# Start of a one-layer RG-LRU, attention and FFN kernel: gain vector through ScalarE's queue, ones first on GpSimd, twelve warm-up products, first weights in two transfers

## The reference, cut to what matters

```python
def rms_norm(x, g):
    y = x * lax.rsqrt(jnp.mean(x * x, axis=-1, keepdims=True) + EPS)
    return y * g

h = rms_norm(x, mix_norm_g[0])
proj = h @ w_in[0]                       # 1024 -> 2560
xr, yg, q, k, v = jnp.split(proj, splits, axis=-1)
...                                      # conv, RG-LRU, attention, norms
x = x + mixed @ w_out[0]
hf = rms_norm(x, ffn_norm_g[0])
up = causal_depthwise_conv(hf @ w_up[0], ffn_conv_w[0], ffn_conv_b[0])
gate, val = jnp.split(up, 2, axis=-1)
return x + (jax.nn.gelu(gate) * val) @ w_down[0]
```

## Time and profile before

| what | before |
|---|---|
| median of 3 runs | 295.36 us (295.22 to 295.43) |
| the profiled execution | 295.82 us |
| its span, first to last instruction | 294.0 us |
| TensorE busy | 287.8 us, 98% of the span |
| VectorE, ScalarE, GpSimd busy | 242.3, 201.0, 11.8 us |
| moved by DMA | 52.23 MB, mean 178 GB/s |

### The profile page before, as it was taken

How to read it: one execution, slowest core, us unless ns; L and a number is a source line. 1 busy time by engine, 2 the same in 40 slices (tenths; PEclk the granted TensorE clock), 3 DMA queues, 4 the chain that set the end, 5 groups by cost and what they waited for, 6 DMA issues and landing times.

```text
span 294.0 us, 4948 instructions
## 1 busy us (share of the span) xinstructions
PE 287.8 (98%) x1618; PEld 248.7 (85%) x1618; DVE 242.3 (82%) x443; ACT 201.0 (68%) x378; POOL 11.8 (4%) x29
## 2 busy tenths in 40 slices
PE   6999999999999999999999999999999999999996
PEld 6688999898788899888888888888888888888885
DVE  2798798898899777999978888888788888888864
ACT  4894498989695488888666666676666666776540
POOL 4000000900000000000000000000000000000000
PEclk9999999999999999999999999999999999999999
DMA  7999941231256702664746444464736544200004
GB/s 278 424 424 421 393 149 56 91 143 54 91 173 255 281 9 60 226 246 183 283 148 246 168 168 165 159 237 143 285 143 236 186 157 162 115 0 0 0 0 145
DMA packets 8111, 52.23 MB, mean 178 GB/s; under 512 B 928, under 2 KB 1312, under 8 KB 2080
## 3 DMA queue, kind: packets, MB, share of 16 engines
q1 hardware_dynamic: 7920, 51.50, 46.8%
q0 software_dynamic: 176, 0.53, 0.5%
HBM read 50.98 MB, written 1.05 MB: 177 GB/s over the span
## 4 chain that ended last, share of the span: by engine, by line
PE 94%; ACT 3%; DVE 1%; issue 1%; POOL 0%; ACTq 0%; POOLq 0%
PE bank L1353 25%; PE bank L1033 15%; PE bank L1034 15%; PE bank L1037 15%; PE bank L1357 13%; PE bank L1103 2%; PE bank L1083 1%; PE bank L1142 1%; ACT w_hi L361 1%; PE bank L1256 1%; PE bank L1169 1%; PE bank L1114 1%; DVE h_both L939 1%; PE bank L1320 1%; PE bank L1136 1%
## 5 line engine op out<-in xcount | busy, mean ns | idle before, releaser
L684 DVE TENSOR_TENSOR w_lo<-raw,w_hi 128x1024 fp32r<-128x1024 f32 x93 | 111.0, 1221 | 7.4 <-ACT w_hi L361 6.3
L361 ACT ACTIVATE w_hi<-raw 128x1024 fp32r<-128x1024 f32 x85 | 86.8, 1058 | 4.9 <-PE bank L1037 4.5
L1353 PE MATMUL bank<-h_both,w_hi 128*128 128x512 f32 x336 | 83.7, 391 | 0.6 <-ACT w_hi L361 0.6
L1353 PEld LDWEIGHTS bank<-h_both,w_hi 128*128 128x128 f32 x336 | 61.6, 188 | 12.6 <-issue 0.8
L1357 PEld LDWEIGHTS bank<-h_both,w_lo 128*128 128x128 f32 x336 | 45.8, 190 | 3.3
L1357 PE MATMUL bank<-h_both,w_lo 128*128 128x256 f32 x336 | 46.8, 282 | 0.0
L603 ACT ACTIVATE tanh_a<-bank 128x256 f32<-128x256 f32 x44 | 16.8, 381 | 40.8 <-PE bank L1357 39.9
L1033 PE MATMUL bank<-w_hi,act_hi 128*128 128x512 f32 (+1 forms) x90 | 34.8, 387 | 0.0
L1034 PE MATMUL bank<-w_lo,act_hi 128*128 128x512 f32 (+1 forms) x90 | 34.8, 387 | 0.0
L1037 PE MATMUL bank<-w_hi,act_lo 128*128 128x512 f32 (+1 forms) x90 | 34.6, 384 | 0.0
L611 ACT ACTIVATE xc<-ygate,par 128x256 f32<-128x256 f32 x44 | 26.2, 595 | 3.2 <-DVE ygate L961 3.2
(11 more groups left out here) (168 smaller groups left out, 402.8 us busy)
## 6 DMA issues: line engine op xcount, KB each, us to landing
raw<-in_stream_dram SPq DMA_DIRECT2D x47, 1024.0 KB, 4.8
x_tok<-in_x_dram SPq DMA_DIRECT2D x2, 512.0 KB, 5.1
out_dram<-x_tok SPq DMA_DIRECT2D x3, 256.0 KB, 2.3
p_T<-in_gates_dram POOLq DMA_DIRECT2D x1, 512.0 KB, 9.3
out_dram<-x_tok SPq DMA_DIRECT2D x2, 128.0 KB, 2.2
par<-in_params_dram SPq DMA_DIRECT2D x1, 117.0 KB, 6.7
mix_g<-in_params_dram POOLq DMA_DIRECT2D x1, 4.0 KB, 5.7
```

The costliest lines, as they stand in the source:

```text
L361: act.activation(w_hi[u % RING][:, :], raw_unit(u), ACT.Copy).then_inc(hi_done, 1)
L684: dve.tensor_tensor(w_lo[u % RING][:, :], raw_unit(u), w_hi[u % RING][:, :].bitcast(F32), ALU.subtract).then_inc(lo_done, 1)
L1353: pe.matmul(acc[:, :], whi[:, kc, :], h_both[:, kc, :, :].rearrange("p b t -> p (b t)"), start=kc == 0, stop=False)
```

## The change

The gain's transfer is issued by ScalarE as its first instruction, and no longer by GpSimd, so the memset of `ones` is GpSimd's first instruction in the block. `WARM_UP` goes from 10 to 12. The first 1 MB of weights goes as two transfers of 512 KB, one for each unit, with a semaphore of its own for unit 0 (`first_landed`), which `q_plain` waits for. The users of unit 1, and of all later units, still wait for `raw_landed[0]` and the others.

```diff
-WARM_UP = 10
+WARM_UP = 12
...
+        first_landed = sem("first_landed")
...
             sp.dma_start(x_tok[:, 0, :], x_t[0]).then_inc(x_landed[0], 16)
-            sp.dma_start(raw[0][:, :], stream[0]).then_inc(raw_landed[0], 16)
+            sp.dma_start(raw_unit(0), stream[0][:, 0:UNIT]).then_inc(first_landed, 16)
+            sp.dma_start(raw_unit(1), stream[0][:, UNIT:2 * UNIT]).then_inc(raw_landed[0], 16)
             sp.dma_start(x_tok[:, 1, :], x_t[1]).then_inc(x_landed[1], 16)
             sp.dma_start(par[:, :], params).then_inc(par_landed, 16)
...
         @block.gpsimd
         def _(pool):
-            pool.dma_start(mix_g[:, :], params[:, MIX_G:MIX_G + KC]).then_inc(gain_landed, 16)
             pool.memset(ones[:, :], 1.0).then_inc(ones_done, 1)
...
+            act.dma_start(mix_g[:, :], params[:, MIX_G:MIX_G + KC]).then_inc(gain_landed, 16)
             act.wait_ge(consts, 1)
             act.activation(warm_out, eps, ACT.Sqrt).then_inc(warm, 1)
...
             def q_plain(m, kc):
 
-                pe.wait_ge(raw_landed[0], 16)
+                pe.wait_ge(first_landed, 16)
                 pe.wait_ge(plain_done, PLAIN.index((m, kc)) + 1)
```

## The result

The changed kernel takes 296.36 us (median of 7 runs, 296.20 to 296.44) against 295.43 for the kernel before (7 runs, 295.04 to 295.52) on the same chip: ratio 1.0034, interval 1.0025 to 1.0043. It is 0.93 us slower. I had forecast 0.4 us faster, 294.5 to 295.5. The sign was wrong.

The account below looks back on a forecast made before the run. TensorE, nearly always busy, passes opening changes through to the end. ScalarE free at 8.38 and tile 1 at 8.2 put the square at 8.4 instead of 8.81: 295.36 - 0.4 = 294.95 us, range 294.5 to 295.5.

Parts of the forecast that it names:

- What decides: Opening, ScalarE: the new start of the square of tile 1, less 8.81, gives the change in time; -0.4 us.
- The step that failed: First 1 MB of weights: splitting it delays unit 1 and tile 1 by at most 0.2 us; 0.1 taken.
- My slower rival: Opening: late clock rise, +1.6 us (296.95), or transfer parts paid one after the other, +1.8; slower cases together 0.08.
- Tile 1 at 8.2: Opening DMA: tile 1 of x lands at 8.2 us instead of 8.6, bounds 8.0 to 8.9.
- ScalarE free at 8.4: Opening: with faster transposes, ScalarE finishes its four blocks of tile 0 at 8.38 us, before squaring tile 1.
- GpSimd's queue, 0.4 us on tile 1: Opening DMA: without GpSimd's 32 packets tile 1 gains between 0 and 0.4 us; 0.4 taken.
- GpSimd's start: Opening, GpSimd: the memset of `ones` starts between 0.80 and 1.31 us; 1.0 taken.
- The rival in which GpSimd starts no earlier: Opening: GpSimd starts at 1.31 us, warm-up ends at 6.67; only -0.2 us, 295.15; chance 0.14.
- Clock: Transposes of tile 0: clock rises at 7.1 us, 5.8 after work begins; they span under 1.5 us instead of 1.72.
- The gain on ScalarE: Opening, ScalarE: issuing `mix_g` is hidden in idle time; its rows cost tiles 0 and 1 0.1 us each.
- The late clock: Pause between warm-up and tile 0's transposes: the clock's rise waits for a new unbroken stretch; +1.6 us, 296.95.

Follow-up runs that it names:

- e14: The change without the split, the gain's transfer issued later on ScalarE, behind its table load and first root: 294.99 us against 295.30 for the kernel before, ratio 0.9993.
- e6: The kernel before, unchanged but for an empty line, profiled again as a typical execution: 295.37 us.
- e13: The change with the two halves laid contiguous in memory, nothing else altered: 295.29 us against 295.33 for the kernel before.
- e10: Kernel before with `ones` first, 12 warm-up products, the gain on GpSimd behind the memsets, two transfers from contiguous halves: 295.89 us, ratio 1.0018.
- e16: The change with contiguous halves and the gain's transfer on SyncE's queue right behind tile 0 of x: 296.58 us, ratio 1.0044 to the kernel before.
- e1: Kernel before with only the split into two transfers of 512 KB: 296.62 us against 295.25, ratio 1.0044.
- e2: Kernel before with only the gain's transfer moved to ScalarE, ten warm-up products, no split: 295.32 us against 295.25; 2 of 12 executions at 296.75 and 296.85.
- e9: Kernel before with two transfers of 512 KB, each of 64 whole rows of 8 KB: 299.95 us, ratio 1.0123.
- e3: The change without the split: 295.42 us against 295.25 for the kernel before.
- e5: The change without the split, the gain's transfer on GpSimd behind the two memsets: 295.20 us against 295.26 for the kernel before.
- e8: Kernel before with only the split, the host laying unit 1 behind unit 0 so each half is contiguous: 295.81 us, ratio 1.0013.
- e12: Kernel before with `raw[1]` split into two transfers instead of `raw[0]`: 295.21 us against 295.33.
- e18: Repeat of the change without the split, the gain issued on ScalarE behind table load and first root: 295.00 us against 295.23 for the kernel before, ratio 0.9990.
- e11: Kernel before with only the split, unit 1's half of each row fetched before unit 0's: 296.48 us, ratio 1.0030.

## Why the prediction was wrong, point by point

*What decides.* I had taken the start of the square of tile 1 as the thing that carries the time. As a rule it holds. Its start and the device time of the same profiled execution:

| kernel | square of tile 1 | time | difference |
|---|---|---|---|
| e14 | 8.16 | 294.90 | 286.74 |
| e6, kernel before | 8.53 | 295.37 | 286.84 |
| e13 | 8.54 | 295.26 | 286.72 |
| kernel before, first profile | 8.81 | 295.82 | 287.01 |
| e10 | 9.14 | 296.03 | 286.89 |
| the change | 9.49 | 296.36 | 286.87 |
| e16 | 9.92 | 296.58 | 286.66 |
| e1 | 10.10 | 296.82 | 286.72 |

Over 1.9 us the time follows one for one, within 0.25 us of 286.8. The other profiles fit as well, but for two: e2 (8.99 and 296.75), in which the clock was late, and e9 (11.74 and 299.96), in which unit 1 itself came only at 10.87. But the rule is not a wait in every row. Where tile 1 lands early, TensorE does not wait for its square's path: in e3 tile 1 is scaled by 10.86, and the first transpose runs at 11.15, behind TensorE's own products. There the square and TensorE's products both follow the same four blocks of ScalarE, and so move together.

*The step that failed* is the one on two transfers of 512 KB: "at most 0.2 us later for unit 1 and for tile 1; I take 0.1". Measured: 0.9 us within the change (with and without the split), 1.4 on the kernel before. I had priced rows of 4 KB by x's rows, which follow each other in memory without a gap. The halves' rows lie 8 KB apart, with the other half between them, and I read the edit `stream[0][:, 0:UNIT]` as a matter of size and not of pitch. In e1 those rows took 0.27 us instead of 0.16; in the change it is 16 x 1.06 x 4096 bytes / 293 GB/s = 0.24. That the layout is the cause within the change is shown by e13; why such rows are slow is open. As an end of a bound, x's row was the wrong kind of row, and the trace of before had no row of the right kind: there the bound should have stayed open above. My slower rival came with a mechanism (parts paid one after the other) that would cost 1.8 us; the loss had its place but not its cause. The Trainium skill (DMA: Bandwidth & Descriptors, "Anatomy of one DMA") has its fixed 2.0 us a transfer from transfers that GpSimd issues; these are SyncE's. They are not paid one after the other here: in e13 tile 1 lands behind two transfers at 8.5 us, as it does behind one in e3 (1.73 + 6.8).

*The path behind it.* Tile 1 at 8.2 (8.0 to 8.9 as bounds): it landed at 9.5. ScalarE free at 8.4: by its four blocks from 7.46 it was free at about 8.6. The later of the two decided, as said, and it was the other one. I had put no price on unit 1's own path. It landed at 8.2 instead of 7.2, so its low part and TensorE's product with it came later too. The changed kernel:

```profile
8.94 1.23 DVE L686 TENSOR_TENSOR w_lo<-raw,w_hi 128x1024 fp32r<-128x1024 f32 x1
...
10.22 0.49 PE L1069 MATMUL bank<-w_lo,h_both 128*128 128x512 f32 x1
...
11.28 0.39 PE L1071 MATMUL bank<-w_hi,h_both 128*128 128x512 f32 x1
```

and e6, the kernel before:

```profile
7.96 1.23 DVE L684 TENSOR_TENSOR w_lo<-raw,w_hi 128x1024 fp32r<-128x1024 f32 x1
...
10.04 0.39 PE L1067 MATMUL bank<-w_lo,h_both 128*128 128x512 f32 x1
...
10.97 0.39 PE L1069 MATMUL bank<-w_hi,h_both 128*128 128x512 f32 x1
```

The last product ahead of tile 1's transposes starts 0.3 us later. As an estimate from these rows, about 0.3 of the 0.93 us would have been lost even with tile 1 on time.

*GpSimd's queue, 0.4 us on tile 1.* Not found. Tile 1 lands at 8.3 with the gain on GpSimd (e5), at 8.5 in the kernel before and in e3, and the 0.4 of the first profile is not in the second. The guess of the Trainium skill (DMA: Bandwidth & Descriptors, "Latency and other measured facts") and my reading of one execution had supported each other. No run supports either: e3 has no transfer on GpSimd in its opening, and its tile 1 lands no earlier.

*GpSimd's start.* I took 1.0 between 0.81 and 1.31; it is 0.81. All of the 0.5 us that precede the transfer in the kernel before belong to the transfer. The rival in which GpSimd starts no earlier is out.

*Clock.* The transposes of tile 0 came at 0.92 us, under my 1.5. But a second profile of the kernel before has them at 0.93 too: I counted a gain against one slow execution that the median does not have. Nor does the rise follow the beginning of work by a fixed 5.8 us. With the same twenty passes from 2.32 us, the warm-up's weight loads span 4.34 us in the first profile and in e6, 3.97 in e8, 3.77 in e12 and 3.72 in e9. In these three the upper level was reached inside the warm-up, though the granted clock reads 1.00 over the stretch in all of them. The forecast of -0.4 against the median should have been about -0.15 from e6's rows; e14 and e18, which have all of the change but the split, and ScalarE's issue later, give -0.2 to -0.3.

*The gain on ScalarE.* Hidden, as said (e3 against before: 0.2 us at most, interval around 1).

*The late clock* was a real danger in the place I named, with ten products (4 of 24 runs lose that time). With twelve it did not come in 44 executions.

## What to carry to other kernels

When a transfer is cut, look at what each part reads: parts of 4 KB out of rows of 8 KB took 1.5 (the change) to 1.7 times (e1) as long per byte, for the half that came first. If the first unit is needed early, have the host lay it contiguous, and measure it, since even that was not always free here. Compare a forecast with a typical execution: this one's profile was of a run 0.4 us above the median, as much as the whole effect sought. And in an opening, ask of each transfer which one is behind it in the queue: the first half, whose early landing was worth nothing, delayed the second half and the tile behind both.

## What the runs showed of the hardware

- Rows of 4 KB at a pitch of 8 KB: 200 GB/s at a DMA share of 0.83 for the half that is fetched first (0.27 us a row), against 410 for contiguous rows or rows of 8 KB (0.16 us for 4 KB). The half fetched second is faster, 312 to 320 GB/s. It moves with the order (e11) and with the megabyte (e12: 239 GB/s).
- With the gain's issue on ScalarE at the same time as x's (the change itself) the same split ran at 293 GB/s instead of 200 between 3.8 and 5.4 us. Why is open, as is the drop to 295 GB/s of contiguous halves in e16 and to 292 in e10. The stretch of the change:

```profile
3.80:5.40 1.60, 1.60 (x9) 1.60 (x9) 0.70 (x2) 0.71 (x2) 0.18 (x2) 1.00 1.06 293
```

- GpSimd's first memset starts at 0.81 us, but a transfer as its first instruction only at 1.31, and it takes 0.73 us more to issue. On ScalarE the same issue starts at 0.81 and takes 0.41 us.
- Two transfers to 64 of the 128 partitions each, with whole rows of 8 KB, ran at 226 GB/s between 3.8 and 7.8 us (e9); the second landed at 1.84 + 8.9 = 10.7 us.
- With 20 warm-up passes from 1.06 us and a pause of about 1 us behind them (both profiles), 4 of 24 executions lost 1.5 us or more; the one that was profiled ran at the lower clock level up to about 10.5 us, though the granted clock in its stretches reads 1.00.
